# Sliding-window attention in a three-pass fp32 decoder kernel: scores and values of two head pairs issued back to back, every second step

## The reference, cut to what matters

```python
def swa_mixer(h, kb, vb, w_q, sinks, rel_table, w_out):
    q = (h @ w_q).reshape(B, NB, BLOCK, SWA_KV_HEADS, SWA_GROUP, SWA_HEAD_DIM)
    s = jnp.einsum('bnqhgd,bnkhd->bnhgqk', q, kb).astype(jnp.float32) * (SWA_HEAD_DIM ** -0.5)
...
    s = jnp.where(mask[None, :, None, None], s + bias, NEG)
    sink = sinks.astype(jnp.float32).reshape(SWA_KV_HEADS, SWA_GROUP, 1, 1)
    m = jnp.maximum(jnp.max(s, axis=-1, keepdims=True), sink)
    p = jnp.exp(s - m)
    p = p / (jnp.sum(p, axis=-1, keepdims=True) + jnp.exp(sink - m))
    o = jnp.einsum('bnhgqk,bnkhd->bnqhgd', p.astype(vb.dtype), vb)
    return o.reshape(B, T, SWA_Q_HEADS * SWA_HEAD_DIM) @ w_out
```

## Time and profile before

| | us |
|---|---|
| median of 3 runs | 973.66 (972.47 to 973.87) |
| profiled execution: span, first to last instruction | 972.1 |
| PE busy | 964.1 |
| DVE busy | 659.3 |
| ACT busy | 492.2 |
| mean granted clock of PE, as a share of full speed | 0.998 |
| the stage of this change, first S to the fifth projection piece | 307.17 to 357.39 |

### The profile page before, as it was taken

The page is one execution under the profiler, slowest core; times in us unless marked ns, Lnnn a source line. Parts: engine busy times, 40 slices in busy tenths (PEclk is TensorE's granted clock), DMA queues, the critical chain, the costliest instruction groups (busy, mean ns, idle before and its releaser), DMA issues.

```text
span 972.1 us, 13083 instructions
## 1 busy us (share of the span) xinstructions
PE 964.1 (99%) x5366; PEld 828.2 (85%) x5366; DVE 659.3 (68%) x934; ACT 492.2 (51%) x589; POOL 59.4 (6%) x128
## 2 busy tenths in 40 slices
PE   9999999999999999999999999999999999999997
PEld 8888888888889878888888889988888888888886
DVE  5877776555569967656666658767766766566665
ACT  5465554444447855444444444455564544444454
POOL 2441000000001001000000013000000000000000
PEclk9999999999999999999999999999999999999999
DMA  8664667677463326766765556443266465555551
GB/s 257 201 201 133 208 178 229 218 199 227 173 216 97 122 88 191 224 194 213 200 213 202 187 162 216 156 167 117 83 229 214 152 216 173 194 195 181 190 193 54
DMA packets 115251, 176.57 MB, mean 182 GB/s; under 512 B 5548, under 2 KB 78200, under 8 KB 115192
## 3 DMA queue, kind: packets, MB, share of 16 engines
q1 hardware_dynamic: 115016, 175.54, 56.5%
q10 hardware_dynamic: 176, 0.20, 0.1%
HBM read 174.03 MB, written 1.70 MB: 181 GB/s over the span
## 4 chain that ended last, share of the span: by engine, by line
PE 98%; DVE 1%; DMA 0%; ACT 0%; issue 0%; POOL 0%; SPq 0%; ACTq 0%; DVEq 0%
PE ps L367 94%; PE ps L371 3%; DMA x<-in_x 0%; DVE RR L1242 0%; DVE wlo L1234 0%; ACT RR L2152 0%; ACT xs L2149 0%; DVE M L1234 0%; SPq L2939 0%; DVE x L1242 0%; POOL st L2763 0%; ACT M L2152 0%; DVE dg L1238 0%; DVE M L2129 0%; DVE x L1234 0%
## 5 line engine op out<-in xcount | busy, mean ns | idle before, releaser
L367 PE MATMUL ps<-whi,RR 128*128 128x512 f32 (+1 forms) x1556 | 397.2, 387 | 0.0
L1234 DVE TENSOR_TENSOR wlo<-raw,whi 128x1024 fp32r<-128x1024 f32 (+1 forms) x323 | 372.9, 1197 | 26.5 <-ACT whi L2152 26.2
L2152 ACT ACTIVATE whi<-raw 128x2048 fp32r<-128x2048 f32 (+1 forms) x161 | 301.1, 1873 | 163.8 <-PE ps L367 136.6
L367 PEld LDWEIGHTS ps<-whi,RR 128*128 128x128 f32 x1556 | 283.9, 188 | 55.7 <-issue 0.9
L367 PE MATMUL ps<-RR,whi 128*128 128x512 f32 (+1 forms) x1264 | 261.7, 351 | 0.0
L367 PEld LDWEIGHTS ps<-RR,whi 128*128 128x128 f32 x1264 | 201.3, 191 | 26.7 <-issue 1.5
L367 PE MATMUL ps<-wlo,RR 128*128 128x512 f32 (+1 forms) x778 | 220.5, 385 | 0.0
L367 PEld LDWEIGHTS ps<-wlo,RR 128*128 128x128 f32 x778 | 144.2, 188 | 29.4 <-DVE wlo L1234 0.2
L1234 DVE TENSOR_TENSOR M<-M,ps 128x512 f32<-128x512 f32 (+1 forms) x57 | 38.7, 682 | 172.8 <-ACT M L2152 168.5
L367 PEld LDWEIGHTS ps<-RR,wlo 128*128 128x128 f32 x1016 | 138.3, 191 | 9.1 <-DVE wlo L1234 0.7
L367 PE MATMUL ps<-RR,wlo 128*128 128x256 f32 x1016 | 144.7, 283 | 0.0
(11 more groups left out here) (109 smaller groups left out, 420.2 us busy)
## 6 DMA issues: line engine op xcount, KB each, us to landing
raw<-in_w_up SPq DMA_DIRECT2D x32, 1024.0 KB, 6.3
raw<-in_w_down SPq DMA_DIRECT2D x32, 1024.0 KB, 5.4
raw<-in_w_ff SPq DMA_DIRECT2D x32, 1024.0 KB, 5.2
raw<-in_w_in SPq DMA_DIRECT2D x23, 1024.0 KB, 5.2
raw<-in_a_w_in SPq DMA_DIRECT2D x10, 1024.0 KB, 5.5
raw<-in_a_w_out SPq DMA_DIRECT2D x4, 1024.0 KB, 5.1
raw<-in_b_w_q SPq DMA_DIRECT2D x4, 1024.0 KB, 5.5
raw<-in_b_w_out SPq DMA_DIRECT2D x4, 1024.0 KB, 5.1
```

The source lines that it names most:

```text
L367: return pe.matmul(out, lhsT, rhs, start=start, stop=stop, skip_group_check=True)
L1234: return dve.tensor_tensor(out, a, b, op)
L2152: return act.activation(out, in_, ACT.Copy, **k)
```

## The change

It alters, for the sliding-window attention alone, the order on PE, DVE and ACT, and the banks:

- `scores` of pairs 2n and 2n+1 are issued back to back, the odd one into banks 2 and 3: pairs 0 and 1 ahead of q2, pairs 2 and 3 after q3, 4 and 5 after q5, 6 and 7 after q7;
- `values` of two pairs are issued back to back: 0 and 1 after q5, 2 and 3 after q7, 4 and 5 after P1, 6 and 7 after P3; in a step that has both, values stand ahead of scores, behind the step's T. The values of pairs 0 and 1, and of 2 and 3, share one bank and are copied and subtracted as one piece of 512 columns;
- T keeps its steps;
- on DVE, `shares` and `soft` change places in even steps, so that the order runs soft(1), shares(0), shares(1), soft(2), and so on; before it was shares(0), soft(1), soft(2), shares(1), soft(3), shares(2);
- query products and values swap banks, and the copy of the transposed probabilities has three buffers in place of two.

```diff
     def sw_v(self, p):
-        return self.M[:, 5120 + 768 * (p % 2):5888 + 768 * (p % 2)].rearrange("p (h k) -> p h k", h=2)
+        return self.M[:, 6912 + 768 * (p % 3):7680 + 768 * (p % 3)].rearrange("p (h k) -> p h k", h=2)
...
+Q_BANKS = {2: 4, 3: 5, 4: 4, 5: 5, 6: 5, 7: 4}
+
+PV_BANKS = {0: 4, 2: 5, 4: 2, 5: 3, 6: 2, 7: 3}
...
+def pv_tile(p):
+    return "pv", p if p > 3 else p // 2
...
     def scores(p):
         tile = ("sc", p)
-        take(tile, 0, 1)
+        take(tile, *((2, 3) if p % 2 else (0, 1)))
...
     def window():
 
         scores(0)
-        yield
         scores(1)
+        yield
         v_turned()
-        for i in range(1, 10):
+        for i in range(2, 11):
             yield
-            if i == 1:
-                turned(0)
-            if i < 7:
+            if i < 10:
+                turned(i - 2)
+            if i % 2 == 0 and i > 2:
+                values(i - 4)
+                values(i - 3)
+            if i % 2 == 0 and i < 8:
+                scores(i)
                 scores(i + 1)
-            if 1 < i < 9:
-                turned(i - 1)
-            if i > 1:
-                values(i - 2)
...
     def window():
 
         for i in range(11):
 
-            if i == 1:
-                shares(0)
+            if i % 2 == 0 and 0 < i < 9:
+                shares(i - 1)
+            if i % 2 == 0 and i > 2:
+                lows(i - 4)
             if i < 8:
                 soft(i)
-            if 3 < i:
+            if i in (8, 10):
                 lows(i - 3)
-            if 1 < i < 9:
+            if i % 2 and i < 9:
                 shares(i - 1)
-            if i == 3:
-                lows(0)
             yield
...
     def turned(p):
         tile = ("pt", p)
-        for w in due(K.full(tile), *([K.full(("pv", p - 2))] if p >= 2 else [])):
+        for w in due(K.full(tile), *([K.full(pv_tile(p - 3))] if p >= 3 else [])):
...
-            if 3 <= i:
+            if i % 2 == 0 and i > 2:
+                highs(i - 4)
+            if i in (8, 10):
                 highs(i - 3)
```

More of the change, by code:

```diff
@@ L306, in line_runs, with pv_cols, pv_parts @@
     return [(m, n, dil, col, kind == "next") for m, n, col, kind in runs]
+def pv_tile(p):
+    return "pv", p if p > 3 else p // 2
+def pv_cols(p):
+    a = 0 if p > 3 else 256 * (p % 2)
+    return slice(a, a + 256)
+def pv_parts(oT, p):
+    return [part[:, p:p + (1 if p > 3 else 2), :].rearrange("p k t -> p (k t)") for part in oT]
 def by_parity(a):
@@ L903, in values @@
     def values(p):
-        tile = ("pv", p)
+        tile, cols = pv_tile(p), pv_cols(p)
         v = V.sw_v(p)
         kv = p // 4
-        w_ = take(tile, 2 + p % 2)[:, 0:256]
+        if cols.start == 0:
+            take(tile, PV_BANKS[p])
+        w_ = K.bank(tile)[:, cols]
         for w in due(K.empty(("pt", p)), K.empty(("kv",))):
@@ L917, in values @@
             t = mm(w_[rows[h], 128:256], v1, v[:, h, 256:384], False, True)
-        t.then_inc(*K.filled(tile))
+        if p > 3 or p % 2:
+            t.then_inc(*K.filled(tile))
     def v_turned():
-        b = take(("kv",), 2)
+        b = take(("kv",), 6)
         for w in due(K.empty(("vt",))):
@@ L930, in window @@
         scores(0)
+        scores(1)
         yield
-        scores(1)
         v_turned()
-        for i in range(1, 10):
+        for i in range(2, 11):
             yield
-            if i == 1:
-                turned(0)
-            if i < 7:
+            if i < 10:
[5 more added lines that the diff above has]
+                scores(i)
                 scores(i + 1)
-            if 1 < i < 9:
-                turned(i - 1)
-            if i > 1:
-                values(i - 2)
     def q_products():
@@ L949, in q_products @@
                 tile = ("q", f // 128 + i)
-                b = take(tile, 4 + i)
+                b = take(tile, Q_BANKS[tile[1]])
                 t = weights_stand(b[:, 0:256], j, hi, lo, cols[i], hT, range(8), h_ready(2), True, True)
@@ L967, in projection @@
                 t = weights_move(K.bank(tile), j, hi, lo, slice(0, 512), o_parts, slice(c * 128, c * 128 + 128),
-                                 range(k0, k0 + 4), k0, lambda k: K.empty(("pv", k)), k0 == 0, k0 == 4)
+                                 range(k0, k0 + 4), k0, lambda k: K.empty(pv_tile(k)), k0 == 0, k0 == 4)
                 if k0:
@@ L1742, in lows @@
     def lows(p):
+        tile, (hi, lo) = pv_tile(p), pv_parts(oT, p)
         for w in due(K.at("pv_hi", p)):
             dve.wait_ge(*w)
-        tt(oT[1][:, p, :], K.bank(("pv", p))[:, 0:256], oT[0][:, p, :].bitcast(F32), ALU.subtract).then_inc(
-            *K.emptied(("pv", p)))
+        tt(lo, K.bank(tile)[:, 0:256 if p > 3 else 512], hi.bitcast(F32), ALU.subtract).then_inc(*K.emptied(tile))
     def window():
         for i in range(11):
-            if i == 1:
-                shares(0)
+            if i % 2 == 0 and 0 < i < 9:
+                shares(i - 1)
+            if i % 2 == 0 and i > 2:
+                lows(i - 4)
             if i < 8:
                 soft(i)
-            if 3 < i:
+            if i in (8, 10):
                 lows(i - 3)
-            if 1 < i < 9:
+            if i % 2 and i < 9:
                 shares(i - 1)
-            if i == 3:
-                lows(0)
             yield
@@ L2456, in highs @@
     def highs(p):
-        for w in due(K.full(("pv", p))):
+        tile = pv_tile(p)
+        for w in due(K.full(tile)):
             act.wait_ge(*w)
-        copy(oT[0][:, p, :], K.bank(("pv", p))[:, 0:256]).then_inc(*K.up("pv_hi", p))
+        copy(pv_parts(oT, p)[0], K.bank(tile)[:, 0:256 if p > 3 else 512]).then_inc(*K.up("pv_hi", p))
     def ev_q(p):
```

## The result

The changed kernel takes 976.08 us (median of 5 runs, 975.92 to 977.7), the kernel before, run beside it, 973.06 (5 runs, 972.45 to 973.87). The ratio is 1.0035, with a 95% interval of 1.0024 to 1.0046: slower by some 3 us. The forecast was 3.1 us slower; its level, 976.8, was reckoned from the earlier median of 973.66.

A forecast was written before the change was run, and what follows sets the result against it. PE was taken to bound the kernel, with DVE close behind, then ACT. T(6) 2.8 us later, PE's gain included, plus 0.3 in the tail took the span from 972.1 to 975.2 and the median to 976.8 us; range 974.0 to 978.2.

The forecast's parts named there:

- T(0): Pair 0's transposes on PE: start at 316.84 instead of 315.11, since soft(1) precedes shares(0) on DVE; 2.1 us wait.
- T(2): Pair 2's transposes on PE: start at 327.1, with DVE idling 0.78 us ahead of shares(1) for exps(1).
- The loop: Two pairs, T to T, through PE, ACT's copy and DVE: six terms, 11.6 us, against 11.1 before.
- T(4) and T(6): Transposes of pairs 4 and 6 on PE: at 338.7 and 350.3, the latter 2.8 us later than before.
- The tail: PE from T(6) to the fifth projection piece P4: 10.15 us against 9.83, adding 0.3 us.
- PE's gain: Attention stage on PE: 18 fewer changes of the array's form at 0.17 us each, 3.1 us less work.
- rival 1: PE's gain reaches the end because transposes are ready when PE comes: 970.6 us, chance 0.08.
- Rival 2: DVE has no idle time in the stage, its own work sets T(6): 973.0 us, chance 0.12.
- Rival 3: Loop longer still: dearer second V, late exps(odd) on ACT, late lows(2) for P0; some 978.3 us, chance 0.15.
- Two edits costed at nothing: Banks for S(odd) free about in time; P0's need for lows of pair 2 met, else 1 us more.
- The clock: A falling PE clock was not priced as a rival: granted 1.00 before, waits of 1 to 2 us.

The follow-up runs named there:

- refitted kernel: Changed kernel with DVE's weight low parts between shares(even) and shares(odd), and ACT's order fitted to that: 969.86 us, ratio 0.9971 to the kernel before.
- two experiments: Changed kernel with shares(0) ahead of soft(1) on DVE, 977.24 us; changed kernel with DVE's old order of soft and shares, 981.44 us.
- the third: Changed kernel with DVE's weight low parts moved between shares(even) and shares(odd), ACT and PE as changed: 973.23 us.
- DVE's order as before: Changed kernel with DVE's old order of soft and shares, PE and ACT as changed: 981.44 us.
- scores ahead: Two scores issued ahead of two values on PE in even steps: on the changed kernel 982.01 us, on the refitted kernel 971.89 us.

## Why the prediction was right

**T(0)** was forecast at 316.84, which with the 1.07 of offset is 315.77: it came there to the hundredth. **T(2)** forecast 327.1, measured 326.09 + 1.07 = 327.16; DVE's idle time ahead of shares(1) 0.70 for 0.78. **The loop** forecast 11.6, measured 11.62 and 11.63, and each of its six terms within 0.01. T(4) and T(6), 338.7 and 350.3, came at 338.78 and 350.41. The waits were forecast start to start, 2.1, 1.4, 1.3 and 1.3. The idle times in the rows (1.84, 1.19, 1.03, 1.27) are shorter by their nature, since they begin at the recorded end of the matmul before; in the forecast's measure (315.77 - 312.81 less the usual 0.96, and so on) the waits are 2.00, 1.36, 1.19 and 1.42. **The tail** took 10.11 for 10.15. The sum, +3.1, was +3.13 from S(0) to P4, and the medians differ by 3.0. One number off the path was too large: DVE's idle time for the copy, 0.56 for 0.7.

**PE's gain** was put at 3.1, with the lower bound for the second S or V behind the first (0.65). For V that is right: two take 1.46 (350.18 to 351.64) where one takes 0.81. For S it isn't: two take 1.61 (316.62 to 318.23), so the second costs 0.76. Four times 0.1 make the gain 2.7; the refitted kernel shows 2.71, or 2.84 with what is left of waiting taken out on both sides. The step was mis-sized by 0.3 to 0.4, and it didn't show, because all of PE's gain went into waits; had rival 1 come true, its time would have been that much too low. That the sum agrees to a few hundredths is in this part owed to the gain having no way to the end. The Trainium skill, TensorEngine Tiling (Array Packing), section Tiling Modes, says that a change of mode drains TensorE; the trace agrees in so far as changes cost time, 2.71 to 2.84 us for 18 fewer, some 0.15 to 0.16 each.

**Rival 1** (the gain reaches the end, 970.6) didn't happen, but the refitted kernel is what it described: shares(even) early enough, 969.86. **Rival 2** is excluded by DVE's idle rows. **Rival 3** named three lengthenings of the loop, and none is there.

**Two edits costed at nothing** cost nothing in the changed kernel, but with little margin. S(odd) was said to wait for a bank that comes free in time. The wait that matters is another, for ACT's copy of its query product behind exps(odd - 2), and what covered it was the late T(0) itself: with T(0) early it cost 3.0 us in two experiments and 1.6 in the third. And P0's wait for lows of pair 2, not met here, came to 1.22 us with DVE's order as before, and to 0.30 and 0.28 in the two kernels with scores ahead.

**The clock** was set aside because waits of 1 to 2 us have several us of matmuls between them. In the changed kernel's profile it did stay at 1.00 through the stage, the 1.84 us wait included. The kernel with scores ahead issues the same work up to T(0), has the same 1.84 ahead of it, and was granted 0.50 from 316 to 319 (above); its T(0) and two S:

```profile
315.33 1.09 PE L389 MATMUL ps<-ident,M 128*128 128x128 f32 x6 [1.84 <-DVE M L1259]
316.35 3.09 PE L385 MATMUL ps<-M 64*128 64x128 f32 x16
```

where the changed kernel has 0.92 and 1.68 in the same two rows. So the step left out a cost that the change can meet, and nothing in the profile of before could price it. In the profiled execution of the changed kernel it was not met at all, which is luck; with scores ahead the same fall cost 0.40 at T(2), the rest being covered by DVE's chain. The other executions of the changed kernel have no trace: the one with a mean granted clock of 1.000 took 975.99 us, beside the profiled one's 975.92, and the three with 0.996 or 0.997 took 976.08 to 977.7.

## What to carry to other kernels

Before work is moved on the busiest engine, look at the engine behind it in the stretch concerned, not over the program: a gain on PE is only as large as the slack of whoever feeds it. When an engine's work is regrouped, the orders of the others have to be regrouped with it, and what belongs to no chain (here the weights' parts) goes where they wait. And the largest wait in a profile need not be a cost: follow it into the loop it belongs to, sum the loop, and ask which term can leave it. Read waits start to start as well, since short ones show no idle time.

## What was not expected of the hardware

- Behind a wait of 3.0 us (twice), of 2.65 and of 1.84, PE was granted 0.50 of its clock, 1.2 GHz, from 0.1 to 0.6 us after it had taken up work again: q4's 16 matmuls took 2.90 and 3.27 for 2.01. After another wait of 1.84 us, with the same work ahead of it, after one of 2.12 with DVE as before, and after one of 2.30 in the kernel with scores ahead, the clock stayed at 1.00. So the length of the wait alone did not decide. The Trainium skill, TensorE: Matmul & The Clock Gate, Part 1: The HAM clock gate, describes a gate that halves the clock after idleness and lets it go again with activity, and says of the rise at a kernel's start that its moment varies between runs of one kernel; the two waits of 1.84 show the like for the fall.
- A second group of 64-row matmuls directly behind the first costs 0.76 us, a second group of 64-column ones 0.65, which is six times the 0.109 of a 128-column transpose, their columns alone.
